# Squared latent tiles summed on VectorE before one product with ones, instead of one product with ones per tile

## The chip, the cores and the metric

The kernel runs on one core of one Trainium2 chip. The metric is the device time of one execution in microseconds (us); the time of a kernel is the median of its runs. TensorE (PE) does the matrix products, VectorE (DVE) and ScalarE (ACT) the elementwise work, GpSimd (POOL) a part of the subtractions, and SyncE (SP) issues the weight loads.

## What is computed

Two models of two layers each run one after the other on 512 tokens of width 1024, all in fp32. The change lies in the first of them, in the MLA branch of `_layer`:

```python
h = x @ w_in
(c_q, c_kv, k_rope, ...) = _split_last(h, IN_SPLITS)      # c_q is 384 wide, c_kv 256
q  = (_rms_norm(c_q,  q_norm)  @ w_qb).reshape(...)
kv = (_rms_norm(c_kv, kv_norm) @ w_kvb).reshape(...)

def _rms_norm(x, g):
    y = x * rsqrt(mean(x * x, axis=-1) + 1e-6)
    return y * g
```

Beside this branch a layer has a memory attention (softmax over 256 memory tokens), a stick-breaking and a decayed-softmax attention, gates for all of them, and a merge. There are two layers of this kind, so the two norms above are computed four times in all.

## The kernel before, in words

Activations lie feature-major: a tile is 128 features by 512 tokens (128x512). c_q is three such tiles (n = 0, 1, 2) and c_kv two (n = 3, 4). A mean over features is a sum over partitions, which is done on TensorE: the square of a tile is multiplied by a 128x128 matrix of ones, and the products of all tiles of a norm are added up in one PSUM bank. After it every partition holds the sum for its token. Every other fp32 product with weights is split into three (`L1654`, `L1655`, `L1656`: low times high, high times low, high times high) in the fp32r type; the product with ones is a plain fp32 matmul, which the trace shows as two instructions.

The whole program is one list of steps, written by a planner (`plan`, line 304), and each engine's program walks this list in order and takes from it what is its own. An engine's instructions are thus in the order of the list, and a wait holds everything behind it on that engine. The planner counts a cost in ns per step (`cost_of`, line 244: 693 for one k-step of a 512-column product, that is three matmuls; 860 for a `squares` step; 0 for everything that TensorE doesn't do). `alongside` (line 687) weaves two generators by these costs: the fill (here `mla_proj`, the projections of the MLA branch) and the main (here the memory attention). It issues a main step when the fill's cost so far, times the main's total over the fill's total, has caught up with the main's cost so far, and a due time has passed. The totals come from a first run of the planner. The memory attention thus runs beside `mla_proj`, in the stage that is called `mem` here.

Line 785, `mla_proj`, in order: tiles 0 and 1 from weight `cq0` (8 k-steps each), tile 2 and then tile 3 from `cq1`; first call of the generator `normed` for q; the square of tile 3; tile 4 from `ckr`; second call; the rotary key with the forget gates (`krope`) from `ckr`; the rest of `normed` for q; `normed` for kv is started, and is called once more after each k-step of the gate projection `g0`; then `qb`, `kvb` and the rest. Each tile is followed by a step `raw` (ScalarE copies the bank to SBUF and squares it into a tile `tmp`). `normed` (line 796) puts the steps `squares` (TensorE, line 1754, the product with ones at L1761), `rroot` (ScalarE: Ln and Exp of the sum, shown as L1806), `normed` (VectorE: three operations of a Newton correction, L2139, L2142, L2144, then one multiplication per tile at L2263), and `normhi` (ScalarE rounds each tile to fp32r, L1922, and GpSimd subtracts it, L2584). Its `yield`s say between which steps the caller goes on:

```python
            put("rroot", l=l, b=b, tm=tm, dim=dim)
            yield
            tn = TN.take()
            put("normed", l=l, b=b, tm=tm, tn=tn, dim=dim, grp=grp, gain=gain)
            give(b, tm, tn)
            ready = now() + 5000
            for _ in range(40):
                if now() < ready:
                    yield
            put("normhi", l=l, grp=grp)
```

`krope` on VectorE is two operations (L2269, L2271). Further lines that the prediction names: `turn` is a group of transposes of the memory attention (L1726), `rturn` the transposes of its reciprocals (L1735), which wait for VectorE's L2404; L1692 is a logit product, L1750 a product with the values, L2376 the maximum of a logit tile, L1817 a load of an activation table, L1826 and L2175 or L2570 the splitting of a weight chunk. L2247 is VectorE's part of a gate.

Of the kernel before, what the change touches and what calls it, by code (L numbers as in the profile page):

```python
# [303 lines left out]
def plan(known):  # L304
# [480 lines left out]
    def mla_proj(l, box):  # L785
        sq = []

        def take_tile(w, c0):
            b = yield from gemm("fm", w, c0, c0 + 128, ("x", l), range(8))
            tm = TM.take()  # L790
            put("raw", l=l, n=len(sq), b=b, tm=tm)
            give(b)
            sq.append(tm)
            yield

        def normed(grp, dim, gain):
            b = GR[0].take()
            for n in grp:
                put("squares", l=l, n=n, b=b, tm=sq[n], first=n == grp[0], last=n == grp[-1])
                give(sq[n])  # L800
            tm = TM.take()
            put("rroot", l=l, b=b, tm=tm, dim=dim)
            yield
# [9 lines that stand above are left out]
        w = wnext("cq0")  # L813
        yield from take_tile(w, 0)
        yield from take_tile(w, 128)
        wdone(w)
        w = wnext("cq1")
        yield from take_tile(w, 0)
        b = yield from gemm("fm", w, 128, 256, ("x", l), range(8))
        wdone(w)  # L820
        put("rawcopy", l=l, n=3, b=b)
        give(b)
        norm_q = normed((0, 1, 2), 384, "qn")
        next(norm_q)
        sq.append(TM.take())
        put("rawsquare", l=l, n=3, tm=sq[3])
        yield
        w = wnext("ckr")
        yield from take_tile(w, 0)
        next(norm_q, None)  # L830
        b = yield from gemm("fm", w, 128, 256, ("x", l), range(8))
        put("krope", l=l, b=b)
        give(b)
        rest_of(norm_q)
        wdone(w)
        norm_kv = normed((3, 4), 256, "kvn")
        next(norm_kv)
        yield
        g0 = gate("g0", l, "mla", l)
        for x in g0:  # L840
            if x is not None:
                box["u"] = x
            next(norm_kv, None)
            yield
        rest_of(norm_kv)
        w = wnext("qb")
        for c in range(2):
            b = yield from gemm("fm", w, 128 * c, 128 * c + 128, ("nq", l), range(3))
            put("qnope", l=l, c=c, b=b)
            give(b)  # L850
            tick()
            yield

        def turn_rope(part, src):
            b, t2 = GR[0].take(), TM.take()
            put("rope1", l=l, part=part, src=src, b=b, tm=t2)
            give(b, t2)

        b = yield from gemm("fm", w, 256, 384, ("nq", l), range(3))
        tm = TM.take()  # L860
        put("qb", l=l, b=b, tm=tm)
        give(b)
        wdone(w)
        turn_rope("k", None)
        yield
        w = wnext("kvb")
        for c in range(2):
            b = yield from gemm("fm", w, 128 * c, 128 * c + 128, ("nkv", l), range(2))
            put("knope", l=l, c=c, b=b)
            give(b)  # L870
            tick()
            yield
        turn_rope("q", tm)
        give(tm)
        for i in range(4):
            b = yield from gemm("kvv", w, 256, 512, ("nkv", l), range(2), tile=i)
            put("mlav", l=l, i=i, b=b)
            give(b)
            tick()
            yield  # L880
        wdone(w)
        e_ = TM.take()
        put("foxgate", l=l, e=e_)
        give(e_)
# [356 lines left out]
    for l in range(2):  # L1241
        box, tail = {}, iter(())
        run(project(l, "A", box, first))
        first = {}
# [112 lines left out]
def build(nc, ctx, a, out):  # L1357
# [184 lines left out]
    def tensor_program(e):  # L1542
# [50 lines left out]
        for s in STEPS:  # L1593
# [160 lines left out]
            elif k == "squares":  # L1754
                b = s["b"]
                w.wait_ge(d_tail, d_tail.at("tail"))
                if s["first"]:
                    for g, v in b.free():
                        w.wait_ge(g, v)
                w.wait_ge(a_fn, a_fn.at(("square", s["tm"])))  # L1760
                t = e.matmul(bank(b), C("ones"), tm(s["tm"]), start=s["first"], stop=s["last"])  # L1761
                t.then_inc(aux.sem, aux.mark(b, ends=(s["tm"],)))
            elif k == "rope1":
                b = s["b"]
                w.wait_ge(d_tail, d_tail.at("tail"))
                for g, v in b.free():
                    w.wait_ge(g, v)
                if s["part"] == "k":
                    w.wait_ge(v_copy, v_copy.at(("krope", s["l"])))
                    src = kp  # L1770
                else:
                    w.wait_ge(v_copy, v_copy.at(("qb", s["src"])))
                    src = tm(s["src"])
                t = e.matmul(bank(b), C("rot16"), src, start=True, stop=True)
                t.then_inc(aux.sem, aux.mark(b))
            elif k == "rope2":
                b = s["b"]
                for g, v in b.free():
                    w.wait_ge(g, v)
                w.wait_ge(a_copy, a_copy.at(("pair", s["src"])))  # L1780
                t = e.matmul(bank(b), C(ROT[s["br"]][0]), tm(s["src"]), start=True, stop=True)  # L1781
                t.then_inc(aux.sem, aux.mark(b))
            elif k in ("qsquares", "dsquares"):
                b = s["b"]
                for g, v in b.free():
                    w.wait_ge(g, v)
                sq = s["sq"] if k == "qsquares" else s["ta"]
                w.wait_ge(a_fn, a_fn.at(("square", sq)))
                t = e.matmul(bank(b), C("bones"), tm(sq), start=True, stop=True)
                t.then_inc(aux.sem, aux.mark(b))  # L1790
            elif k == "vturn":
                b = s["b"]
                for g, v in b.free():
                    w.wait_ge(g, v)
                w.wait_ge(a_copy, a_copy.at(("vcopy", s["tm"])))
                for i in range(4):
                    c = slice(128 * i, 128 * i + 128)
                    t = e.transpose(bank(b)[:, c], tm(s["tm"])[:, c], C("ident"))
                t.then_inc(feat.sem, feat.mark(b, ends=(s["tm"],)))
# [331 lines left out]
    def vector_program(e):  # L2131
# [34 lines left out]
        for s in STEPS:  # L2166
# [82 lines left out]
            elif k == "mkv" and s["n"] == 1:  # L2249
# [3 lines left out]
                    w.wait_ge(heado, heado.at(("heado", 0, "mem", 1)))  # L2253
                t = e.tensor_copy(mv[:, c, :], bank(b)[:, 0:256])
                t.then_inc(v_copy.sem, v_copy.mark(("mkv", l, 1, c), ends=(b,)))
            elif k == "normed":
                l, x = s["l"], tm(s["tm"])
                w.wait_ge(d_par1, d_par1.at("par"))
# [503 lines left out]
```

## Time and profile before

| | |
|---|---|
| runs | 1453.92, 1451.4, 1452.3 us; median 1452.3 |
| profiled execution | 1448.79 us, span 1447.0 |
| mean granted clock of TensorE | 0.988 |
| busy: PE, DVE, ACT, POOL | 95%, 59%, 50%, 26% of the span |

The span goes from the first to the last instruction; 1.8 us of the profiled execution lie outside it. PE's busy share counts a matmul from its start to its modelled end, and such matmuls overlap: two 512-column matmuls of the same kind start about 0.23 us apart and are 0.39 us long each. So the start times are what to read, not the durations. The granted clock is 1.00 at 2.4 GHz and 0.50 at 1.2 GHz.

### The profile page before, as it was taken

The page shows a single profiled execution, that of the slowest core. Times are in us where ns is not written, and L with a number is a line of the kernel's source. Part 1 is how long each engine was busy: PE and PEld are TensorE (multiplying, and loading weights), DVE is VectorE, ACT ScalarE, POOL GpSimd, SP SyncE. Part 2 cuts the span into 40 slices and gives each one's busy share as a digit, 9 for nine tenths or more (in the row PEclk, how much of TensorE's full clock was granted, in tenths as well). Part 3 has the DMA queues.
Part 4 walks back from the last instruction along what each step waited for, and adds up shares of the span by engine and source line. Part 5 has one row for each costly group of instructions (what it writes and reads, how often), then busy time and mean ns, then how long its engine had stood idle before and what let it go on. Part 6 is the DMA issues. An engine that isn't in the chain of part 4 may idle for free.

```text
span 1447.0 us, 20166 instructions
## 1 busy us (share of the span) xinstructions
PE 1378.0 (95%) x7530; PEld 1061.5 (73%) x7530; DVE 858.3 (59%) x1505; ACT 728.8 (50%) x1557; POOL 379.6 (26%) x273
## 2 busy tenths in 40 slices
PE   7999999999989999999998899999899999999897
PEld 7867688778787677887776876766667876766665
DVE  4655536557562553365587685458756665558655
ACT  4554447555244554566554464445444554536443
POOL 2232131345132321313564111421102111421111
PEclk9999999999999999999999999999999999999999
DMA  6413551126343221112255523612323342520311
GB/s 235 117 31 92 113 142 48 50 72 226 102 161 62 57 89 59 59 48 66 77 218 174 131 65 67 124 59 52 102 67 88 103 102 64 113 65 23 117 52 59
DMA packets 185895, 135.67 MB, mean 94 GB/s; under 512 B 91334, under 2 KB 166726, under 8 KB 185798
## 3 DMA queue, kind: packets, MB, share of 16 engines
q1 hardware_dynamic: 182022, 120.22, 30.8%
q10 hardware_dynamic: 3776, 14.16, 2.6%
q8 instruction: 61, 1.00, 0.3%
q14 instruction: 36, 0.29, 0.1%
HBM read 122.03 MB, written 12.32 MB: 93 GB/s over the span
## 4 chain that ended last, share of the span: by engine, by line
PE 74%; DVE 13%; ACT 9%; issue 2%; POOL 1%; DMA 0%; DVEq 0%; ACTq 0%; POOLq 0%
PE pb L1654 19%; PE pb L1656 18%; PE pb L1655 18%; PE pb L1750 5%; PE pb L1692 5%; PE pb L1726 4%; ACT prob L1806 4%; ACT tmp L1806 2%; DVE wl L2175 2%; DVE prob L2426 2%; ACT wh L1826 1%; PE pb L1781 1%; PE pb L1735 1%; PE pb L1698 1%; DVE small L2412 1%
## 5 line engine op out<-in xcount | busy, mean ns | idle before, releaser
L2570 POOL TENSOR_TENSOR wl<-wr,wh 128x512 fp32r<-128x512 f32 x178 | 251.4, 1413 | 724.8 <-ACT wh L1826 721.0
L1654 PE MATMUL pb<-xh,wl 128*128 128x512 f32 (+1 forms) x880 | 349.5, 397 | 6.4 <-DVE wl L2175 3.1
L1656 PE MATMUL pb<-xh,wh 128*128 128x512 f32 (+1 forms) x880 | 326.0, 370 | 0.0
L1655 PE MATMUL pb<-xl,wh 128*128 128x512 f32 (+1 forms) x880 | 325.8, 370 | 0.0
L2175 DVE TENSOR_TENSOR wl<-wr,wh 128x512 fp32r<-128x512 f32 x208 | 171.5, 827 | 173.3 <-ACT wh L1826 173.0
L1826 ACT CAST wh<-wr 128x512 fp32r<-128x512 f32 (+1 forms) x386 | 220.1, 606 | 34.0 <-PE pb L1656 15.1
L1654 PEld LDWEIGHTS pb<-xh,wl 128*128 128x128 f32 x880 | 168.4, 191 | 62.0 <-issue 31.8
L1656 PEld LDWEIGHTS pb<-xh,wh 128*128 128x128 f32 x880 | 168.1, 191 | 29.1
L1655 PEld LDWEIGHTS pb<-xl,wh 128*128 128x128 f32 x880 | 168.9, 192 | 23.2 <-issue 2.9
L1806 ACT ACTIVATE tmp<-pb,cst 128x512 f32<-128x512 f32 (+3 forms) x128 | 83.0, 648 | 81.5 <-PE pb L1656 35.5
L1654 PE MATMUL pb<-wh,xl 128*128 128x256 f32 (+1 forms) x320 | 108.9, 340 | 10.0 <-DVE wl L2175 7.9
L1726 PEld LDWEIGHTS pb<-cst,prob 128*128 128x128 f32 x768 | 93.3, 142 | 31.0 <-issue 11.4
L1726 PE MATMUL pb<-cst,prob 128*128 128x128 f32 x768 | 111.7, 276 | 4.1 <-DVE small L2401 2.2
L2059 ACT COPY prob<-pb 128x512 f32<-128x512 f32 (+3 forms) x128 | 61.4, 480 | 106.2 <-PE pb L1726 105.6
L1806 ACT ACTIVATE prob<-prob,small 128x512 f32<-128x512 f32 (+3 forms) x128 | 75.9, 594 | 72.0 <-DVE small L2389 71.9
L1656 PE MATMUL pb<-wh,xh 128*128 128x256 f32 (+1 forms) x320 | 105.3, 329 | 0.0
L1655 PE MATMUL pb<-wl,xh 128*128 128x256 f32 (+1 forms) x320 | 105.2, 329 | 0.0
L1806 ACT ACTIVATE prob<-pb,small 128x512 f32<-128x512 f32 (+1 forms) x96 | 58.2, 614 | 90.5 <-DVE small L2412 50.9
L2591 POOL TENSOR_TENSOR yl<-tmp,yh 128x512 fp32r<-128x512 f32 x28 | 36.1, 1291 | 244.1 <-ACT yh L2071 240.5
L2447 DVE COPY prob<-pb 128x512 f32<-128x512 f32 (+3 forms) x128 | 70.0, 551 | 43.3 <-PE pb L1726 42.8
L1654 PE MATMUL pb<-wh,yl 128*128 128x512 f32 (+1 forms) x176 | 69.5, 395 | 8.7 <-DVE wl L2175 7.0
L1654 PEld LDWEIGHTS pb<-wh,xl 128*128 128x128 f32 x320 | 61.3, 192 | 21.6 <-DVE wl L2175 8.2
(200 smaller groups left out, 2326.5 us busy)
## 6 DMA issues: line engine op xcount, KB each, us to landing
wr<-w_in SPq DMA_DIRECT2D x39, 1024.0 KB, 5.4
wr<-w_out SPq DMA_DIRECT2D x14, 1024.0 KB, 5.0
wr<-w_in SPq DMA_DIRECT2D x48, 256.0 KB, 4.6
wr<-w_branch SPq DMA_DIRECT2D x48, 128.0 KB, 2.3
x<-prob SPq DMA_DIRECT2D x12, 512.0 KB, 3.2
wr<-w_mem_kv SPq DMA_DIRECT2D x4, 1024.0 KB, 5.8
prob<-x ACTq DMA_DIRECT2D x2, 2048.0 KB, 11.0
wr<-w_out SPq DMA_DIRECT2D x16, 256.0 KB, 4.2
```

The source lines that it names most:

```text
L1654: e.matmul(ps, ll, rh, start=start, stop=False)
L1655: e.matmul(ps, lh, rl, start=False, stop=False)
L1656: t = e.matmul(ps, lh, rh, start=False, stop=stop)
L1692: t = e.matmul(bank(b)[:, 0:128 * (hi - lo)], lhs, rhs, start=True, stop=br != "mla")
L1726: t = e.transpose(bank(b)[:, c], probs(p)[:, c], C("ident"))
L1750: t = e.matmul(bank(b)[64 * half:64 * half + 64, lo:hi], v_[:, j, vc:vc + 64], turns(s["t"][half])[:, j, lo - 256 * ih:hi - 256 * ih], sta ...
L1806: return e.activation(o, i, f, bias=C("zero", 0, i.shape[0]) if bias is None else bias, scale=scale, **kw)
L1826: e.copy(wh[:, j % 2, c0:c1], wr[:, j % 2, c0:c1]).then_inc(w_hi.sem, w_hi.mark((j, c)))
L2059: t = e.copy(turns(t_)[:, lo:hi, 128 * i:128 * i + 128], bank(b)[:, 0:128 * (hi - lo)].rearrange("p (j c) -> p j c", c=128))
L2175: t = e.tensor_tensor(wl[:, j % 2, c0:c1], wr[:, j % 2, c0:c1], wh[:, j % 2, c0:c1].bitcast(F32), ALU.subtract)
L2447: t = e.tensor_copy(turns(t_)[:, lo:hi, 128 * i:128 * i + 128], bank(b)[:, 0:128 * (hi - lo)].rearrange("p (j c) -> p j c", c=128))
L2570: t = e.tensor_tensor(wl[:, j % 2, c0:c1], wr[:, j % 2, c0:c1], wh[:, j % 2, c0:c1].bitcast(F32), ALU.subtract)
```

## The change

`normed` first has VectorE add the other squared tiles of the group into the first one (steps `sqsum`: two for q, one for kv), and gives the caller its turn; when it is called again, it puts one `squares` step for the sum, and `rroot`. Everything behind it in `normed` thus comes one call later than before. The product with ones waits for VectorE's sum and no longer for ScalarE's square.

```diff
         def normed(grp, dim, gain):
+            for n in grp[1:]:
+                put("sqsum", tm=sq[grp[0]], add=sq[n])
+                give(sq[n])
+            yield
             b = GR[0].take()
-            for n in grp:
-                put("squares", l=l, n=n, b=b, tm=sq[n], first=n == grp[0], last=n == grp[-1])
-                give(sq[n])
+            put("squares", l=l, b=b, tm=sq[grp[0]])
+            give(sq[grp[0]])
             tm = TM.take()
             put("rroot", l=l, b=b, tm=tm, dim=dim)
             yield
...
             elif k == "squares":
...
-                if s["first"]:
-                    for g, v in b.free():
-                        w.wait_ge(g, v)
-                w.wait_ge(a_fn, a_fn.at(("square", s["tm"])))
-                t = e.matmul(bank(b), C("ones"), tm(s["tm"]), start=s["first"], stop=s["last"])
+                for g, v in b.free():
+                    w.wait_ge(g, v)
+                w.wait_ge(v_fn, v_fn.at(("sqsum", s["tm"])))
+                t = e.matmul(bank(b), C("ones"), tm(s["tm"]), start=True, stop=True)
...
+            elif k == "sqsum":
+                x = tm(s["tm"])
+                w.wait_ge(a_fn, a_fn.at(("square", s["tm"])))
+                w.wait_ge(a_fn, a_fn.at(("square", s["add"])))
+                w.wait_ge(v_fn, v_fn.n)
+                t = e.tensor_tensor(x, x, tm(s["add"]), ALU.add)
+                t.then_inc(v_fn.sem, v_fn.mark(("sqsum", s["tm"]), ends=(s["add"],)))
```

## Rows read from the trace of the kernel before

**Rows 1.** The page: busy time of the engines, and the chain that ended last.
```profile
PE 1378.0 (95%) x7530; PEld 1061.5 (73%) x7530; DVE 858.3 (59%) x1505; ACT 728.8 (50%) x1557; POOL 379.6 (26%) x273
...
PE 74%; DVE 13%; ACT 9%; issue 2%; POOL 1%; DMA 0%; DVEq 0%; ACTq 0%; POOLq 0%
```
**Rows 2.** The instructions of L1761, the products with ones: count, ns min/median/max.
```profile
L1761 PE MATMUL pb<-tmp,cst x20: 590/592/593, 77.2 to 488.0; 128*128 128x512 f32 x20
```
**Rows 3.** Timeline of PE, layer 0: start us, length us, instructions merged, idle before.
```profile
77.24 2.73 PE L1761 MATMUL pb<-tmp,cst 128*128 128x512 f32 x6
79.90 1.13 PE L1692 MATMUL pb<-tbias,setB 64*128 64x256 f32 x8
...
91.82 0.38 PE L1726 MATMUL pb<-cst,prob 128*128 128x128 f32 x2
...
92.73 0.38 PE L1726 MATMUL pb<-cst,prob 128*128 128x128 f32 x2
...
94.34 1.88 PE L1761 MATMUL pb<-tmp,cst 128*128 128x512 f32 x4
96.06 0.60 PE L1726 MATMUL pb<-cst,prob 128*128 128x128 f32 x4
```
**Rows 4.** Timeline of DVE, layer 0, around both norms.
```profile
87.00 1.07 DVE L2142 SCALAR_TENSOR_TENSOR scr<-scr,tmp 128x512 f32<-128x512 f32 x1
...
88.83 2.08 DVE L2263 SCALAR_TENSOR_TENSOR setB<-setB,par,tmp 128x512 f32<-128x512 f32 x3
...
94.54 0.74 DVE L2269 TENSOR_SCALAR fz<-pb,par 36x512 f32<-36x512 f32 x1 [1.88 <-PE pb L1656]
95.21 0.67 DVE L2271 COPY setB<-pb 128x512 f32<-128x512 f32 x1
...
97.74 0.69 DVE L2139 SCALAR_TENSOR_TENSOR scr<-pb,tmp 128x512 f32<-128x512 f32 x1 [0.84 <-ACT tmp L1806]
...
99.91 1.42 DVE L2263 SCALAR_TENSOR_TENSOR setB<-setB,par,tmp 128x512 f32<-128x512 f32 x2
```
**Rows 5.** Timeline of DVE: a 128x512 fp32 operation of two SBUF tiles.
```profile
54.89 0.69 DVE L2208 TENSOR_TENSOR setA<-setA 128x512 f32<-128x512 f32 x1 [1.40 <-ACT setA L1806]
```
**Rows 6.** The chain of waits in layer 0 from the kv norm to `rturn`.
```profile
96.26 0.70 ACT tmp L1806
...
104.74 1.04 ACT yh L1922 x2
105.80 1.28 ACT L1817
107.09 0.69 ACT u L1806
...
109.55 0.63 PE pb L1735 x4
```
**Rows 7.** Timeline of PE: `rturn` of both layers, layer 1's kv products, a later wait.
```profile
105.79 0.60 PE L1726 MATMUL pb<-cst,prob 128*128 128x128 f32 x4
109.55 0.63 PE L1735 MATMUL pb<-cst,tmp 128*128 128x128 f32 x4 [3.16 <-DVE tmp L2404]
...
486.72 1.88 PE L1761 MATMUL pb<-tmp,cst 128*128 128x512 f32 x4
...
501.92 0.63 PE L1735 MATMUL pb<-cst,tmp 128*128 128x128 f32 x4 [3.16 <-DVE tmp L2404]
...
811.79 0.58 PE L1654 MATMUL pb<-xh,wl 128*128 128x256 f32 x1 [2.86 <-DVE wl L2175]
```
**Rows 8.** Stretches: us, busy us (x instructions) of PE, PEld, DVE, ACT, POOL, clock, DMA, GB/s.
```profile
811.00:818.00 7.00, 6.21 (x30) 6.21 (x30) 6.34 (x17) 3.67 (x8) 0.00 (x0) 0.51 0.85 174
98.00:110.00 12.00, 8.84 (x49) 6.75 (x47) 7.25 (x16) 6.67 (x17) 4.01 (x4) 1.00 0.00 0
```
**Rows 9.** Timeline of POOL in layer 0: a weight chunk and the `normhi` of q.
```profile
85.90 1.62 POOL L2570 TENSOR_TENSOR wl<-wr,wh 128x512 fp32r<-128x512 f32 x1
...
94.19 4.00 POOL L2584 TENSOR_TENSOR yl<-setB,yh 128x512 fp32r<-128x512 f32 x3 [1.53 <-ACT yh L1922]
```

## The prediction

> **What bounds the kernel now.** I began with the page: TensorE is busy 95% of the span and carries 74% of the chain that ended last, so a TensorE product that goes is worth something unless another engine ends the stretch it stands in [rows 1]. Then the line of the products with ones: 20 instructions, two to a product, so ten products: three for q and two for kv in each of two layers [rows 2]. Then the timelines around them. In layer 0 the q products start at 77.24 and the next work at 79.90, with no idle time around them; the kv products go from 94.34 to 96.06, again without a gap on either side [rows 3]. So far TensorE is the bound. Last I read the chain behind the kv products: it leaves TensorE at 96.26 for ScalarE's Ln and Exp and comes back only at 109.55, at `rturn`, where TensorE has waited 3.16 us [rows 6, 7]. Between the end of the kv products and `rturn` the time is thus set by ScalarE and VectorE, 109.55 - 96.06 = 13.5 us of it. Layer 1 repeats this to the hundredth: kv products at 486.72, `rturn` at 501.92, after 3.16 us [rows 7].
>
> **What is removed.** Of q's three products two go: (79.90 - 77.24) x 2/3 = 1.77 us. Of kv's two one goes: (96.06 - 94.34) / 2 = 0.86 us [rows 3]. All of it lies on the path: 2.63 us per layer, 5.3 in all. If all the rest were free, the kernel would gain that.
>
> **What is added for q.** Two additions on VectorE, at 0.69 us each by the row of two SBUF tiles [rows 5]. The one product that is left stands 8 k-steps (8 x 0.68 us) further on, behind the whole of tile 4. The sum is ready long before, so this costs nothing. It would cost at most these 1.4 us if VectorE were late; but VectorE idles between its jobs here. ScalarE's square of tile 3 has to wait for the first addition, since it takes over the tile that this one frees; nobody needs that square for over 5 us.
>
> **What the later step does.** This is the heart of the matter. The second call of `normed` for q now puts `squares` and `rroot`, and the third part (`normed` on VectorE, `normhi`) comes only when `mla_proj` asks for the rest, behind `krope`. There the planner's clock stands still, and all of it is put at once. VectorE's order behind the end of the `krope` product then is: two operations of `krope`, three Newton operations, three multiplications for q, and only then the one addition for kv. Before, the six q operations ran beside the `krope` product, from before 87.0 to 90.9 [rows 4], where VectorE had time. TensorE's order behind the same product, followed through the planner's costs: one `turn` of two transposes, one k-step of `g0`, and then the kv product, which waits for the addition. (The pacing changes a little: three steps of 860 less in the fill's total raise the ratio, and a few main steps come one k-step earlier. I followed them to the end of the stage and found none that comes to a bank or a copy too early.)
>
> Price, layer 0. TensorE comes to the kv product at 94.34 plus a turn and a k-step, which by the spacing of two such turns is 92.73 - 91.82 = 0.91 us [rows 3]: at 95.25. VectorE starts `krope` at 94.54, and its copy ends at 95.88; the three Newton operations take 99.91 - 97.74 = 2.17, the three multiplications 2.08, the addition 0.69 [rows 4, 5], with steps of 0.03 between them: the sum is there at about 100.9. TensorE waits 100.95 - 95.25 = 5.7 us, with everything behind it in its order: a turn, the gate products, the next logits. ScalarE is held too, at the first `normhi` cast until the first q tile is there (98.8), and then runs at VectorE's pace to 100.8; behind it there are only the root of kv, which waits for TensorE anyway, a copy and a weight chunk that is due 15 k-steps later. Bounds of this wait: 5.5 us if each step is as short as its shortest row, and 6.5 if two operations are stretched as L2142 was, to 1.07 from 0.69, while GpSimd worked at 85.90 [rows 4, 9]. I take 5.7, since GpSimd's `normhi` work [rows 9] can start only at 99.4, and touches only the last operation or two.
>
> Here a rule of the Trainium skill speaks against the change ("GPSIMD Engine Reference", 1. Specifications): GpSimd's SBUF interfaces are shared with VectorE and contend with VectorE instructions that have two SBUF inputs. The addition and the multiplications are such instructions. By the rule the last two would take up to 1.07 us, and the wait 6.5 instead of 5.7; by the plain rows it stays at 5.7. That row of 1.07 agrees with the rule, but `krope` and L2139 ran at their usual length beside GpSimd's 94.19 to 98.19.
>
> **Clock.** Behind a wait of 2.86 us at 811 us TensorE was granted 0.51 over the next 7 us; the wait of 3.16 us before `rturn` left it at 1.00 [rows 7, 8]. A wait of 5.7 us is longer than both, so I expect the lower of the two levels, 1.2 GHz, behind it. The kv product then takes 1.72 instead of 0.86: +0.86 us. Whatever else TensorE does slowly until `rturn` is covered by the wait there. The bounds are 0 and, if the stretch is the whole 7 us long, the 7 x 0.49 = 3.4 us of work lost in it less the 2 us of cover: 1.4. The Trainium skill ("TensorE: Matmul & The Clock Gate", Part 1, What's actually happening) says that the throttled state is the default and activity lifts it; by that rule alone the 3.16 us wait might have dropped the clock as well, which the trace does not show.
>
> **What comes back.** Between the end of the kv product and `rturn` the chain is ScalarE's and VectorE's. One item of it moves: `normhi` for kv, 104.74 to 105.80 in the chain, stands before the gate's table load (L1817) and tanh [rows 6]. With the kv norm one k-step later and the gate's last k-step unchanged, its due time passes only when the gate step is already put, so it falls behind the tanh: the chain is shorter by 105.80 - 104.74 = 1.06 us. Bounds: 0 (it stays where it was) and 1.1; I take 1.1, since the order of steps decides it and not a duration. The wait at `rturn` goes from 3.16 to about 2, still enough for TensorE's slow clock.
>
> **Sum.** Per layer -2.63 + 5.7 + 0.86 - 1.1 = +2.8, for two layers +5.7 us (before rounding, 5.66). On the profiled execution, 1447.0 span and 1.8 around it, that is 1448.8 + 5.7 = 1454.5. The median of the runs lies 3.5 us above this execution, and the change sits in two fixed places, so I add it to the median: 1452.3 + 5.7 = 1458.0. With the least of all terms, 2 x (-2.63 + 5.5 + 0 - 1.1) = +3.5; with the most, 2 x (-2.63 + 6.5 + 1.4 - 0) = +10.5. Own range of this case: 1455.8 to 1462.8.
>
> **Rivals.**
> 1. *The wait at `rturn` swallows the new one.* TensorE waits 3.16 us there already. If `rturn`'s time hung on something that doesn't move with the kv product, each layer would lose only 5.7 - 2.63 - 3.16 = -0.1: no change, 1452.1. For it: the waits are alike in size. Against it: the chain runs through the kv root without a break, 96.26 to 109.55 [rows 6]. Chance 0.18.
> 2. *Faster: the kv sum is early.* If VectorE did the kv addition ahead of q's six operations (or these stayed beside the `krope` product), the addition would end at 95.88 + 0.7 = 96.6 or, in an order with `krope` behind it, before TensorE comes: a wait of at most 1.4 us. It decides from a wait under 2.63 us on. With none, the time is 1452.3 - 5.3 = 1447.0. For it: the step was given a turn of its own, which does spare q all waiting. Against: in the list the addition stands behind `krope` and behind the rest of q. Chance 0.09.
> 3. *Costlier: nothing comes back, and the clock stays low beyond `rturn`.* `normhi` stays in front of the tanh and a second slow stretch follows: the upper sum, 1462.8. For: 7 us at 0.51 in the trace [rows 8]. Against: cover of 2 us. Chance 0.10.
>
> That the change doesn't do what it says (the number of products) I don't count apart: 4 products with ones are sure from the diff.
>
> **Numbers.** My case has 0.63. No change is what lies within 0.2%, 2.9 us. Slower: 0.63 + 0.10 = 0.73; same 0.18; faster 0.09. The range must hold 8 in 10: from rival 1 up to the top of my own case, 1451.5 to 1463.
>
> **What would show it.** L1761 with 8 instructions. A wait of 5 to 6.5 us before the second of each layer's L1761 pairs, released by VectorE's new addition; right ahead of that addition L2139, L2142, L2144 and three L2263 without a gap behind L2271. The granted clock near 0.5 behind it. `normhi` (L1922) behind the gate's tanh, and `rturn` with some 2 us of wait. No wait at q's L1761. I am wrong if the addition for kv stands ahead of L2139 on VectorE, or if `rturn` minus the end of the kv product is not near 12.4 us.

## The result, and the profile after

The kernel after takes 1458.81 us (median of 7 runs, 1455.17 to 1463.64), the kernel before beside it 1452.19 (7 runs, 1448.98 to 1453.92). The ratio is 1.0055, 95% interval 1.0041 to 1.0070: some 8 us slower (5.9 to 10.2); the two medians as they stand differ by 6.6. The forecast was 1458.0. That it lies so close is in part luck: two errors cancel, as the last experiment and the sum below show. The profiled execution of after took 1459.74 us, its span 1457.9, at a mean granted clock of 0.986 (before: 0.988).

The code behind the change stands a few lines lower in after: L1761 is L1763, L1735 is L1738, L2404 is L2413, L2263 (the multiplication) is L2272; L2139, L2142, L2144 are L2141, L2144, L2146. VectorE's new addition is L2263, so L2263 names two different things in the two kernels.

The page of after, busy time and chain [against rows 1]:
```profile
PE 1376.9 (94%) x7518; PEld 1061.2 (73%) x7518; DVE 864.0 (59%) x1511; ACT 730.0 (50%) x1557; POOL 381.0 (26%) x273
...
PE 74%; DVE 14%; ACT 9%; issue 2%; POOL 1%; DMA 0%; ACTq 0%; DVEq 0%; POOLq 0%
```
TensorE has 12 instructions less and VectorE 6 more, as planned. The page shows little else; the waits have to be read from the timelines. The products with ones, L1763 [against rows 2]:
```profile
L1763 PE MATMUL pb<-tmp,cst x8: 590/826/1193, 86.5 to 498.9; 128*128 128x512 f32 x8
```
Eight instructions, four products. A median of 826 and a maximum of 1193 ns against 592 say that half of them ran on a slower clock. TensorE's timeline (start us, length us, instructions merged, idle before) of both layers [against rows 3 and 7]:
```profile
86.55 1.02 PE L1763 MATMUL pb<-tmp,cst 128*128 128x512 f32 x2
...
93.39 0.38 PE L1729 MATMUL pb<-cst,prob 128*128 128x128 f32 x2
...
100.92 2.04 PE L1763 MATMUL pb<-tmp,cst 128*128 128x512 f32 x2 [6.44 <-DVE tmp L2263]
102.75 0.63 PE L1729 MATMUL pb<-cst,prob 128*128 128x128 f32 x2
...
115.82 0.63 PE L1738 MATMUL pb<-cst,tmp 128*128 128x128 f32 x4 [1.64 <-DVE tmp L2413]
...
497.87 2.05 PE L1763 MATMUL pb<-tmp,cst 128*128 128x512 f32 x2 [6.45 <-DVE tmp L2263]
499.71 0.63 PE L1729 MATMUL pb<-cst,prob 128*128 128x128 f32 x2
...
512.78 0.63 PE L1738 MATMUL pb<-cst,tmp 128*128 128x128 f32 x4 [2.06 <-DVE tmp L2413]
```
q's product doesn't wait. kv's waits 6.44 us, then takes 1.84 us instead of 0.86; `rturn` (L1738) waits 1.64 instead of 3.16. What the kv product waits for, on VectorE [against rows 4]:
```profile
93.59 0.74 DVE L2278 TENSOR_SCALAR fz<-pb,par 36x512 f32<-36x512 f32 x1 [1.90 <-PE pb L1659]
94.26 0.67 DVE L2280 COPY setB<-pb 128x512 f32<-128x512 f32 x1
94.86 0.67 DVE L2141 SCALAR_TENSOR_TENSOR scr<-pb,tmp 128x512 f32<-128x512 f32 x1
95.57 0.69 DVE L2144 SCALAR_TENSOR_TENSOR scr<-scr,tmp 128x512 f32<-128x512 f32 x1
96.29 0.69 DVE L2146 SCALAR_TENSOR_TENSOR tmp<-scr,tmp 128x512 f32<-128x512 f32 x1
97.02 2.08 DVE L2272 SCALAR_TENSOR_TENSOR setB<-setB,par,tmp 128x512 f32<-128x512 f32 x3
99.13 1.64 DVE L2263 TENSOR_TENSOR tmp<-tmp 128x512 f32<-128x512 f32 x1
...
114.68 1.00 DVE L2413 COPY tmp<-small 128x512 f32<-128x512 f32 x1
```
The two `krope` operations, q's three Newton operations and three multiplications, then the addition: this is the order that was followed. The addition takes 1.64 us, not 0.69. GpSimd's timeline says what stands beside it, and beside L2413 as well [against rows 9]:
```profile
98.57 4.67 POOL L2593 TENSOR_TENSOR yl<-setB,yh 128x512 fp32r<-128x512 f32 x3 [6.70 <-ACT yh L1924]
...
114.13 2.68 POOL L2593 TENSOR_TENSOR yl<-setB,yh 128x512 fp32r<-128x512 f32 x2 [1.22 <-ACT yh L1924]
```
ScalarE, at the end of the chain to `rturn` [against rows 6]: the table load and the tanh, and the `normhi` casts of kv now behind them:
```profile
111.50 1.28 ACT L1819 ACT_TABLE_LOAD   x1
112.79 0.69 ACT L1808 ACTIVATE u<-pb,cst 128x512 f32<-128x512 f32 x1
113.38 1.12 ACT L1924 CAST yh<-setB 128x512 fp32r<-128x512 f32 x2
```
And the stretches of after around the wait, with the granted clock behind the five engines' busy time [against rows 8]:
```profile
100.00:104.00 4.00, 3.08 (x6) 1.82 (x7) 1.10 (x2) 0.97 (x2) 3.08 (x3) 0.50 0.00 0
...
106.00:116.00 10.00, 8.36 (x45) 6.32 (x44) 6.42 (x13) 6.18 (x16) 3.08 (x3) 1.00 0.00 0
```
The clock is at 0.50 behind the wait until about 105 us and at 1.00 again on the way to `rturn`.

### The profile page after: what moved, and what is told of

The parts are those of the page before. It is cut to its first block, busy times and chain, and to the rows that moved or that the text cites. A ratio compares the mean times of both kernels' runs of the same rounds, so it can differ in the third digit from the quotient of the medians.

```text
span 1457.9 us, 20156 instructions
## 1 busy us (share of the span) xinstructions
PE 1376.9 (94%) x7518; PEld 1061.2 (73%) x7518; DVE 864.0 (59%) x1511; ACT 730.0 (50%) x1557; POOL 381.0 (26%) x273
## 4 chain that ended last, share of the span: by engine, by line
PE 74%; DVE 14%; ACT 9%; issue 2%; POOL 1%; DMA 0%; ACTq 0%; DVEq 0%; POOLq 0%
PE pb L1657 19%; PE pb L1659 17%; PE pb L1658 17%; PE pb L1753 5%; PE pb L1695 5%; PE pb L1729 4%; ACT prob L1808 4%; ACT tmp L1808 2%; DVE prob L2435 2%; DVE wl L2177 2%; ACT wh L1828 1%; PE pb L1783 1%; PE pb L1738 1%; PE pb L1701 1%; PE pb L1619 1%
```

## The experiments

Eleven more kernels were timed beside before, and before was profiled a second time (e12). The letters of the theories are those of the expectations. Throughout, A is: *the place of the steps in the orders of the engines costs the time (of the kv addition, and of q's operations that stand ahead of it), the addition itself does not.* e1, e2, e3 and e6 ran beside one set of 17 executions of before (median 1451.27), e4, e5, e7 and e8 beside another of 27 (1449.94), e9 to e11 beside a third of 19 (1451.88), so the ratios compare better than the medians. Times are medians; "layers" are two stretches of the profile, from a `rturn` before the change's place to one behind it (75.42 to 155.39 and 322.31 to 547.68 us in before), each less the same stretch of before. The last column puts their sum against the second profile of before (e12). Each pair of layers is read from one execution, and TensorE's clock behind `rturn` can add some 1.5 us to a layer in one execution and not in another (see e12 and the last section).

| kernel | median us | ratio [95%] | layers 0, 1 | sum against e12 |
|---|---|---|---|---|
| after | 1458.81 | 1.0055 [1.0041, 1.0070] | +5.5, +4.8 | +6.4 |
| e1 later only | 1458.56 | 1.0050 [1.0032, 1.0067] | +5.6, +6.4 | +8.2 |
| e2 sum only | 1457.87 | 1.0044 [1.0028, 1.0061] | +6.0, +3.9 | +6.1 |
| e3 q's rest beside | 1454.99 | 1.0022 [1.0011, 1.0032] | +3.4, +4.0 | +3.6 |
| e4 both sums early | 1450.78 | 1.0009 [1.0000, 1.0018] | +2.1, +1.5 | -0.2 |
| e5 `normhi` 7500 | 1449.55 | 1.0000 [0.9992, 1.0009] | -0.2, +0.9 | -3.1 |
| e6 q's `normhi` later | 1461.79 | 1.0072 [1.0056, 1.0088] | +7.4, +6.7 | +10.2 |
| e7 busy wait | 1460.21 | 1.0075 [1.0061, 1.0089] | +6.0, +4.4 | +6.5 |
| e8 e4 and 7500 | 1452.23 | 1.0016 [1.0007, 1.0025] | +1.2, +1.7 | -1.0 |
| e9 added as squared | 1447.72 | 0.9972 [0.9960, 0.9983] | +0.1, -1.0 | -4.7 |
| e10 e9 and 9500 | 1444.10 | 0.9953 [0.9941, 0.9966] | -1.0, -2.0 | -6.8 |
| e11 before and 9500 | 1448.26 | 0.9980 [0.9970, 0.9990] | -1.1, +0.1 | -4.8 |
| e12 before again | 1453.82 | one execution | +2.5, +1.3 | 0 |

### e1: the later steps alone

```diff
         def normed(grp, dim, gain):
+            if len(grp) == 2:
+                yield
             b = GR[0].take()
...
             yield
+            if len(grp) == 3:
+                yield
             tn = TN.take()
```


> The products with ones stay one per tile, as before; only the steps behind them come one call later: the Newton operations and multiplications of q behind krope, and the two kv products behind the first k-step of g0. Theory A (the order of the steps is what costs, and the wait for the sum is one of its faces): TensorE has no wait before its kv products, but ScalarE is held at q's normhi until VectorE has done q's six operations, and kv's root stands behind that; kv's Newton operations begin some 4.5 us later than before, the gate's tanh comes out of kv's normhi's way (up to -1.1) and 0.7 us of products are done earlier: +2.5 to +3.5 us per layer, 1457 to 1459 us where before has 1452.2. Theory B (only the wait of TensorE for VectorE's sum costs): within 1 us of before, 1451 to 1453.

Ratio 1.0050, as slow as after, although no product is saved and no addition made. There is hardly a wait at the kv products, as they need only ScalarE's squares; it stands elsewhere. TensorE, then VectorE, then ScalarE of this kernel:
```profile
96.54 1.98 PE L1765 MATMUL pb<-tmp,cst 128*128 128x512 f32 x4 [0.52 <-DVE setB L2275]
...
114.96 0.63 PE L1739 MATMUL pb<-cst,tmp 128*128 128x128 f32 x4 [3.45 <-DVE tmp L2408]
```
```profile
98.57 2.08 DVE L2267 SCALAR_TENSOR_TENSOR setB<-setB,par,tmp 128x512 f32<-128x512 f32 x3
...
102.68 0.69 DVE L2143 SCALAR_TENSOR_TENSOR scr<-pb,tmp 128x512 f32<-128x512 f32 x1 [1.69 <-ACT tmp L1810]
103.40 1.63 DVE L2146 SCALAR_TENSOR_TENSOR scr<-scr,tmp 128x512 f32<-128x512 f32 x1
```
```profile
99.36 1.94 ACT L1926 CAST yh<-setB 128x512 fp32r<-128x512 f32 x3 [5.24 <-DVE setB L2267]
101.21 0.68 ACT L1810 ACTIVATE tmp<-pb,cst 128x512 f32<-128x512 f32 x1
```
ScalarE's Ln for kv (101.21) is queued behind q's three casts, and they wait for VectorE's multiplications. So kv's root, and with it `rturn`, is late by the same VectorE chain; TensorE pays in several small waits and a longer one at `rturn`. Shown: the later steps, without any wait for a sum, cost 7.3 us in all; a part of it is slow clock behind `rturn` (0.50 over some 3 us in layer 0 and 6 us in layer 1). They are not the whole cost of after, though: after has 5.3 us less of products and is no faster, so that the wait for the sum costs some 6 us more (an estimate: 8.0 + 5.3 - 7.3).

### e2: the sum alone, at the old places

```diff
                 give(sq[n])
-            yield
             b = GR[0].take()
```


> The sum on VectorE and one product, but no later step: the product stands directly behind the additions. Theory A: TensorE waits about 1.5 us for q's two additions (they stand behind the gated output's operation on VectorE) and 2.3 us for kv's one (behind krope's two operations), up to 0.9 more where GpSimd works on q's tiles beside the addition; against -2.63 removed: +1 to +2 us per layer, 1454 to 1456.5. Theory B as for A here. A third view (the additions are hidden beside other work whatever their place): 1447.

Ratio 1.0044, more than expected. Both products now wait for an addition that is put right ahead of them:
```profile
83.97 1.10 PE L1762 MATMUL pb<-tmp,cst 128*128 128x512 f32 x2 [2.60 <-DVE tmp L2262]
...
100.39 1.10 PE L1762 MATMUL pb<-tmp,cst 128*128 128x512 f32 x2 [2.33 <-DVE tmp L2262]
```
The two waits, 4.9 us, alone are more than the 2.63 saved, and in layer 1 both products also run slowly behind them (2.05 and 1.53 us long). So the later step did serve its purpose for q, whose product waits for nothing in after; it was too little for kv, and by e1 it delays the rest of q.

### e3 and e6: two ways of taking q's rest out of the way

e3 asks for q's rest after the first k-step of the `krope` product. e6 keeps it where after has it, but puts q's `normhi` some k-steps later, so that GpSimd isn't at work beside the addition.
```diff
e3
-        b = yield from gemm("fm", w, 128, 256, ("x", l), range(8))
+        b = yield from beside_norm(gemm("fm", w, 128, 256, ("x", l), range(8)), norm_q, (1,))
e6
-        rest_of(norm_q)
+        next(norm_q, None)
...
             next(norm_kv, None)
+            next(norm_q, None)
             yield
+        rest_of(norm_q)
```


> The changed kernel, but q's rest is asked for after the first k-step of the krope product, so that VectorE's six operations for q run beside that product again; the kv addition still stands behind krope's two operations. Theory A: the wait before the kv product falls from 6.4 us to about 1.2 (the addition ends some 2.1 us behind the product, TensorE arrives 0.9 behind it), the clock stays at its upper level: 1448 to 1450. If instead the loss came from the wait on the sum as such, or from the pacing of the attention steps, it stays near 1459.

> The changed kernel, but q's normhi (ScalarE's casts and with them GpSimd's subtractions) is put some five k-steps later, so that GpSimd is idle when VectorE does the kv addition. Theory C (GpSimd's work stretches the addition from 0.69 to 1.64 us): the addition takes 0.69 us, the wait falls from 6.4 to 5.5 us, and the kernel is 2 us faster than the changed one, 1456 to 1458. Rival: the addition is long for its own sake (two operands and an output in the same buffer), 1.64 again, and the time stays at 1459.

e3: ratio 1.0022, less than half of the loss. The kv product still waits 4.28 us and then runs slowly (2.04 us long). q's Newton operations begin only at 88.91 instead of 86.29, as its product comes 8 k-steps later than in before; one Newton operation is stretched to 1.66 us and a weight chunk to 1.76 beside GpSimd, and `krope` begins at 96.07 instead of 94.54. VectorE is the bound of this stretch. e6: the addition is back at its length, and the casts are in the way at another place. VectorE, then ScalarE of e6:
```profile
99.10 0.69 DVE L2265 TENSOR_TENSOR tmp<-tmp 128x512 f32<-128x512 f32 x1
```
```profile
109.87 1.67 ACT L1926 CAST yh<-setB 128x512 fp32r<-128x512 f32 x3
```
0.69 without GpSimd, 1.64 with it, at the same place and with the same neighbours: that GpSimd stretches the addition is shown. The wait falls by as much (5.49 us). But the three casts now stand in ScalarE's chain to `rturn`, which comes at 116.42 instead of 115.82, after a wait of 2.76 us instead of 1.64. At `rturn` the clock falls to 0.50 in both layers of e6 and in neither of after, and that is the larger part of its loss: the stretches behind `rturn` take 46.37 and 46.65 us instead of 45.07 and 45.16. Ratio 1.0072.

### e4 and e8: kv's addition ahead of q's rest

```diff
         next(norm_q, None)
+        norm_kv = normed((3, 4), 256, "kvn")
+        next(norm_kv)
         b = yield from beside_norm(gemm("fm", w, 128, 256, ("x", l), range(8)), norm_q, (1,))
...
-        norm_kv = normed((3, 4), 256, "kvn")
         next(norm_kv)
```
e8 is e4 with kv's `normhi` due 7500 instead of 5000 ns later.

> As the one that asks for q's rest beside the krope product, and kv's addition is put as soon as tile 4 is squared, ahead of krope; the kv product stands where it stood before the change. Theory A: no wait before any product with ones; per layer -2.63 for the products and -0.7 because one more k-step is done under the wait at rturn, whose chain is ScalarE's and VectorE's: -5.3 to -6.6 in all, 1445.5 to 1447. Rival: the gain is lost in the wait at rturn, 1449 to 1451.

> Both sums early, q's rest beside the krope product, and kv's normhi due at 7500: the version that the theories make the fastest. Sum of the two: -5.3 to -6.6 and -2.2, 1443.5 to 1445; if the relief of normhi doesn't come, as the version with both sums early.

No wait at either product and four products: all of the 5.3 us should have been kept. The ratio is 1.0009 for e4, 1.3 us slower than before (0 to 2.6). VectorE and TensorE of e4:
```profile
90.12 1.66 DVE L2159 SCALAR_TENSOR_TENSOR tmp<-scr,tmp 128x512 f32<-128x512 f32 x1
...
93.81 1.79 DVE L2190 TENSOR_TENSOR wl<-wr,wh 128x512 fp32r<-128x512 f32 x1
...
97.45 0.67 DVE L2154 SCALAR_TENSOR_TENSOR scr<-pb,tmp 128x512 f32<-128x512 f32 x1
```
```profile
92.54 1.02 PE L1776 MATMUL pb<-tmp,cst 128*128 128x512 f32 x2
...
109.24 1.09 PE L1751 MATMUL pb<-cst,tmp 128*128 128x128 f32 x4 [3.91 <-DVE tmp L2426]
```
Counted from the `rturn` ahead (74.59 here, 75.42 in before), kv's Newton begins 0.5 us later than in before [rows 4], though its product ends 1.8 us earlier: q's product and root come 8 k-steps late, so that q's operations still fill VectorE, and two operations stretched beside GpSimd (1.66 and 1.79 instead of 0.69 us) add 2.1 us to them. The gain turned into a longer wait at `rturn`, 3.91 us, and the length of that L1751, 1.09 instead of 0.63, tells that the clock had fallen. The expectation missed that VectorE follows close behind TensorE here, and GpSimd's part in it. e8 shortens the casts' part and wins nothing either (1.0016).

### e7: TensorE kept busy in the wait

```diff
+                if s["kv"]:
+                    for _ in range(6):
+                        e.matmul(bank(b), C("ones"), mask_cols("causal", 0, 512), start=True, stop=True)
                 w.wait_ge(v_fn, v_fn.at(("sqsum", s["tm"])))
```


> The changed kernel with six products of ones with a constant (about 5.3 us) put before each kv product, into the bank that this one then starts anew; their result isn't used. They lie inside the wait of 6.4 us. Theory: TensorE's clock then stays at 1.00, the kv product takes 0.9 instead of 1.8 us, and since the chain to rturn starts at its end, the kernel is 1.8 to 2 us faster than the changed one though TensorE does more, 1456 to 1457. Rival: the slow clock was covered, or the added products push the kv product back: 1459 or more.

TensorE in both layers, and the stretch behind the first `rturn`:
```profile
100.82 1.12 PE L1766 MATMUL pb<-tmp,cst 128*128 128x512 f32 x2 [0.42 <-DVE tmp L2266]
...
114.82 0.63 PE L1738 MATMUL pb<-cst,tmp 128*128 128x128 f32 x4 [2.93 <-DVE tmp L2416]
...
512.98 0.63 PE L1738 MATMUL pb<-cst,tmp 128*128 128x128 f32 x4 [2.91 <-DVE tmp L2416]
```
```profile
114.00:118.00 4.00, 3.18 (x12) 2.66 (x13) 2.89 (x4) 0.24 (x1) 1.73 (x2) 0.73 0.21 32
```
The clock holds at the kv product, and in layer 0 `rturn` comes 1.0 us earlier. But the wait at `rturn` is longer too, 2.93 instead of 1.64 us, and behind it the clock falls, where no wait covers it: the next `rturn` comes 46.62 us later instead of 45.07, 1.5 us lost for 1.0 won. In layer 1, after a wait of 2.91 us, it stays at 1.00, and the layer is 0.4 us shorter than in after. The ratio, 1.0075 (1.0061 to 1.0089), shows no gain over after's 1.0055 (1.0041 to 1.0070). So the 0.98 us of the kv product was not won back this way; that the slow stretch behind `rturn` is the whole reason is shown for one layer of one execution only.

### e9: each addition soon behind its square

```diff
+        def added(n0, n):
+            put("sqsum", tm=sq[n0], add=sq[n])
+            give(sq[n])
+            yield
...
         def normed(grp, dim, gain):
-            for n in grp[1:]:
-                put("sqsum", tm=sq[grp[0]], add=sq[n])
-                give(sq[n])
-            yield
             b = GR[0].take()
...
-        yield from take_tile(w, 0)
-        b = yield from gemm("fm", w, 128, 256, ("x", l), range(8))
+        yield from take_tile(w, 0, added(0, 1))
+        b = yield from beside_norm(gemm("fm", w, 128, 256, ("x", l), range(8)), added(0, 2), (4,))
...
-        b = yield from gemm("fm", w, 128, 256, ("x", l), range(8))
+        b = yield from beside_norm(gemm("fm", w, 128, 256, ("x", l), range(8)), added(3, 4), (1,))
```
`beside_norm` steps its second argument once after the k-steps named in its third, counted from 1; what the expectation calls the fifth and the second k-step are the code's fourth and first.

> The kernel after, with each addition put soon behind the square it needs and no later step: tile 1's addition is put after the fifth k-step of tile 1's successor product, tile 2's after the fifth k-step of tile 3's product, kv's after the second k-step of the krope product; both products with ones stand where the kernel before has them. Theory A (the sum itself is cheap; what costs is its place in VectorE's order): no wait of more than 0.1 us at either product with ones, the wait at rturn near 3.2 us as before, the granted clock at 1.00 there as before, and -2.63 us per layer of the removed products, 5.3 us in all: ratio about 0.9964 (-5 us against the kernel before, range -3.5 to -6). Rival D (the stretch is bound by VectorE all along, as the run with both sums early suggested): the removed products are paid back at rturn, whose wait grows by 0.9 us per layer and with it the clock falls behind it: ratio 0.999 to 1.001. Rival E (GpSimd and VectorE's two-input additions get in each other's way): each addition takes 1.64 instead of 0.69 us and pushes VectorE's q operations back, ratio 0.998.

Ratio 0.9972, 4.1 us faster than before (2.5 to 5.8), with the same additions and products as after. TensorE and VectorE:
```profile
92.72 1.02 PE L1776 MATMUL pb<-tmp,cst 128*128 128x512 f32 x2
...
108.23 1.09 PE L1751 MATMUL pb<-cst,tmp 128*128 128x128 f32 x4 [3.65 <-DVE tmp L2426]
```
```profile
89.56 1.77 DVE L2276 TENSOR_TENSOR tmp<-tmp 128x512 f32<-128x512 f32 x1
...
96.26 1.57 DVE L2157 SCALAR_TENSOR_TENSOR scr<-scr,tmp 128x512 f32<-128x512 f32 x1
```
No wait at the products, and the gain lies in the range: A holds. e9 differs from after in two things at once, the place of the additions and that no step is deferred; which of the two is worth how much it doesn't tell. Part of the gain goes where rivals D and E said. The wait at `rturn` grows to 3.65 us (3.44 in layer 1), where the expectation had 3.2, and the clock falls behind it in both layers, where it had 1.00. In layer 0 kv's addition takes 1.77 us beside GpSimd, and kv's second Newton operation, now early enough to meet GpSimd's subtraction for q, takes 1.57 us.

### e5, e10 and e11: `normhi` of kv later

The term "what comes back" by itself, with due 7500 (e5) and 9500 (e11) in the kernel before, and with 9500 in e9 (e10):
```diff
-            ready = now() + 5000
+            ready = now() + (5000 if len(grp) == 3 else 9500)
```
(and 60 instead of 40 tries for 9500).

> The kernel before with one edit: the due time of kv's normhi is 7500 instead of 5000, so that it falls behind the gate's tanh and the reciprocals. Theory: ScalarE's two casts (1.1 us) leave the chain to rturn in both layers, its wait falls from 3.16 to about 2.1 us: -2.2 us, 1450. Rival: something else on the way to rturn is then late (GpSimd's work slows VectorE's copy, as in the changed kernel, where the relief was only 0.3 us): 1451.5 to 1452.5.

> The kernel before with one change: kv's normhi due 9500 instead of 5000 ns later. Due 7500 gave nothing, because GpSimd's subtraction then fell on VectorE's L2404, which took 1.28 instead of 0.44 us. If that collision was the whole reason, the relief of 1.06 us per layer is now seen: L2404 at 0.43 us, wait at rturn 2.1 instead of 3.16, ratio 0.9985 (-2.1 us). If it was not (TensorE is at its own pace right behind rturn or the casts hold up other work of ScalarE), the ratio stays at 1.000.

> The run with each addition behind its square, and kv's normhi due 9500 instead of 5000 ns later, so that its two casts stand behind rturn's work on ScalarE and GpSimd's subtraction behind VectorE's L2404. Theory A with relief: the chain from the kv product to rturn loses the casts (1.06 us), L2404 keeps 0.43 us since GpSimd isn't at work then, the wait at rturn falls to about 2.1 us; -1.1 us per layer more than the same kernel without it: ratio about 0.995 (-7.3 us). Rival: the casts behind rturn hold up ScalarE's exponentials of the next logits, or the kvb products wait for the parts; then it is equal to or slower than the kernel without it (ratio 0.9964 or more).

VectorE and GpSimd of e5, VectorE of e11, then TensorE's `rturn` in layer 1 of e5 and of e11:
```profile
108.03 1.27 DVE L2404 COPY tmp<-small 128x512 f32<-128x512 f32 x1
```
```profile
107.75 2.68 POOL L2584 TENSOR_TENSOR yl<-setB,yh 128x512 fp32r<-128x512 f32 x2 [1.50 <-ACT yh L1922]
```
```profile
108.43 0.43 DVE L2404 COPY tmp<-small 128x512 f32<-128x512 f32 x1
```
```profile
501.29 1.08 PE L1735 MATMUL pb<-cst,tmp 128*128 128x128 f32 x4 [2.97 <-DVE tmp L2404]
```
```profile
499.92 0.63 PE L1735 MATMUL pb<-cst,tmp 128*128 128x128 f32 x4 [2.13 <-DVE tmp L2404]
```
With 7500 the casts leave ScalarE's chain, but GpSimd's subtraction lands on the copy that `rturn` waits for: 1.27 instead of 0.43 us, ratio 1.0000. With 9500 both are out of the way, `rturn` waits 2.12 us, ratio 0.9980 (0.9970 to 0.9990), which holds the 0.9985 expected. In layer 1 of both profiled executions the clock falls behind `rturn`, after 2.97 us in e5 and after 2.13 us in e11 (there 0.50 from some 1 us behind `rturn` on, for some 3 us), which is why their second layers show no gain (+0.9 and +0.1). e10 does both and is the fastest kernel here: 0.9953 against before, 6.8 us (4.9 to 8.6), and each of its executions (1443.76 to 1445.62) is faster than the fastest of before beside it (1447.93).

### e12: the kernel before once more

> The kernel before, unchanged, profiled a second time. Its 19 executions beside the last runs took 1447.9 to 1449.1 us (six, mean granted clock 0.988 to 0.991) or 1451.2 to 1453.2 us (thirteen, 0.984 to 0.989), and the profile of before that all comparisons of traces use is of the lower group (1448.79). Theory: in the upper group TensorE's clock falls to 0.50 behind a wait which the lower one gets through at 1.00; the wait of 3.16 us at rturn is a candidate. If this execution is of the upper group (1451 or more) and the theory holds, one or both rturns are followed by a stretch at 0.50, worth 0.8 to 1.2 us each, and the other places that differ from the first profile are clock dips too. If it is of the lower group, it repeats the first profile within 1 us at every landmark and the candidate stays open.

1453.82 us, so this execution is of the upper group. TensorE at `rturn` of both layers, and the stretches behind the first:
```profile
110.48 1.09 PE L1735 MATMUL pb<-cst,tmp 128*128 128x128 f32 x4 [3.17 <-DVE tmp L2404]
...
505.10 0.98 PE L1735 MATMUL pb<-cst,tmp 128*128 128x128 f32 x4 [3.16 <-DVE tmp L2404]
```
```profile
109.00:112.00 3.00, 1.52 (x6) 1.46 (x7) 2.23 (x7) 0.44 (x2) 0.79 (x1) 0.55 0.09 15
112.00:116.00 4.00, 4.00 (x12) 2.58 (x13) 0.29 (x1) 0.00 (x0) 0.00 (x0) 0.50 0.74 251
```
The same kernel, the same wait to the hundredth [against rows 7 and 8], and this time the clock falls to 0.50 behind it, in both layers. It costs 2.5 us in layer 0 (48.36 against 45.84 us from this `rturn` to the next) and 1.6 in layer 1 (47.34 against 45.76), of which the layer as a whole keeps 1.3. The two layers are 3.8 of the 5.0 us by which this execution's span is longer; another 0.9 lies ahead of the first `rturn`, at 76.34 instead of 75.42. So the profile that the prediction was made from is one of the luckier executions of before: of the 19 beside e9 to e11, six took 1447.9 to 1449.1 us, thirteen 1451.2 to 1453.2. The split is clear in that set only; the 17 and the 27 executions beside the other kernels are not split so: all but the longest of each set lie between 1447.7 and 1453.5 us, with no gap above 1.1. That the other longer executions have the same cause is likely but seen in this one only. It also ran on another chip than the kernels compared with it, so that a difference between chips isn't excluded. In the table, the layers against e12 come much nearer to the ratios of e9 to e11 (-4.7, -6.8 and -4.8 us, measured -4.1, -6.8 and -2.9) than those against the first profile (-0.9, -3.0, -1.0). For e5 they don't: -3.1 by its profile, and 0 measured. But the executions of before beside e4, e5, e7 and e8 have a median of 1449.94, only 1.1 us above the first profile, and there the first profile is the nearer measure for e5 (+0.7) and e7 (+10.4, measured 10.9), while e4 and e8 (measured +1.3 and +2.3) lie between the two.

## Why the prediction was right

The sign and the main mechanism, TensorE's wait for a kv addition that stands behind q's operations, came out as forecast. The median did too, but in part by luck: the terms of the sum did not all hold. The terms of one layer, with layer 1's measured ones (from the `rturn` at 322.31 us of before, 327.81 of after, to that at 547.68 and 557.94):

| step | predicted | measured | how |
|---|---|---|---|
| products removed | -2.63 | -2.63 | half the instructions or less; 1.77 ahead of the kv product, 0.86 at it |
| work moved ahead of the kv product | 0 | +0.97 | TensorE comes to it 163.61 us after the `rturn` instead of 164.41: -0.80 = -1.77 + 0.97 |
| wait for the addition | +5.7 | +6.45 | the timeline |
| slow clock at the product | +0.86 | +0.98 | 499.71 - 497.87 = 1.84, less 0.86 |
| chain to `rturn` | -1.1 | -0.41 | 512.78 - 499.71 = 13.07 instead of 13.48 |
| behind `rturn` | 0 | -0.60 | 45.16 instead of 45.76 us to the next one, which holds one k-step less (29 products of `xh` and `wh` instead of 30) |
| sum | +2.8 | +4.8 | |

- *VectorE's and TensorE's orders* were right to the step. e1 shows that the later steps cost 7.3 us without any addition, e9 that with the additions placed early no product waits for them.
- *The wait* was mis-sized by 0.75 us. The addition takes 1.64 us beside GpSimd; I had taken 0.69 and kept up to 6.5 as a bound. The rule of the Trainium skill that I weighed and set aside ("GPSIMD Engine Reference", 1. Specifications: shared SBUF interfaces) was right, and e6 measures it at 0.95 us for this operation. The counter-evidence I took from the rows was none: of the two `krope` operations and L2139, which kept their length beside GpSimd, none has two SBUF inputs, since all three read a product from PSUM (`pb` in their rows).
- *What comes back* was 0.41 instead of 1.1. The casts did move behind the tanh; but GpSimd's subtraction moved with them, onto L2413 (1.00 instead of 0.43 us). I took the order of the steps for the whole answer and didn't ask what the moved cast sets off on the next engine. e5 and e11 separate the two: nothing, and 2.9 us. By the prediction's own test this part was wrong: from the end of the kv product to `rturn` it is 13.07 us in both layers (115.82 - 102.75), not near 12.4.
- *A missing term*: the turn and the k-step that pass ahead of the kv product lie ahead of a stretch that a chain sets, so they push `rturn` back by 0.97, and only 0.60 returns behind it, where one k-step less is left to do.
- *The clock*: size and place were right in after, 0.98 us for a predicted 0.86. But "the wait of 3.16 us before `rturn` left it at 1.00" was read from one execution; e12 shows the opposite for the same wait. The Trainium skill ("TensorE: Matmul & The Clock Gate", Part 1, What's actually happening: throttled is the default) would have warned of this, and e12's 0.50 behind the wait of 3.17 us agrees with it.
- *Why 1458.0 was still met.* By layer 1's measured terms, after is about 2 x 4.8 = 9.5 us above the first profile of before: 1448.8 + 9.5 = 1458.3. I had 5.7 there, 3.8 too little, and then added it to a median 3.5 us above that profile. The median of before very likely holds the slow clock behind `rturn`, which after's profiled execution, 0.9 us above its median, hasn't (1.64 and 2.06 us of wait, and a clock of 1.00 behind both); that surcharge should not have been carried over. Neither is shown beyond the profiled executions. The two errors cancel.
- *The rivals.* Wait swallowed at `rturn`: no, `rturn` moved by 6.3 us in layer 0. kv sum early: not in after, but it is what e4 and e9 built. e4 got 1450.78 from it, since VectorE was then the bound; e9 got 1447.72, near the 1447.0 that I gave it. Costlier: not as written, since `normhi` did move behind the tanh; but less than half of its relief came back, and the second slow stretch, absent from after's profile, stands behind `rturn` in e1, e2, e6 and e7.

## What to carry to other kernels

Ask of each step that a change defers what stands in line with it on every engine, and who stands behind that: here the deferred calls cost 7.3 us by themselves (e1), against 5.3 us of removed products, and putting each addition soon behind its square, with no call deferred, turned a loss of 0.55% into a gain of 0.28%. Work moved out from under a wait that another engine's chain sets is not free, and a wait may cost the clock behind it; shorten that chain too, and follow the moved instruction to the engine that it feeds. Where a kernel's executions differ by as much as the effect, learn which of them the profile shows before adding a difference to the median.

## What the runs showed of the hardware

- VectorE operations of two SBUF tiles, and copies from SBUF to SBUF, grew by 0.6 to 1.1 us where they met a GpSimd subtraction (1.28 us each when alone): 0.69 to 1.57, 1.64, 1.77 and 1.79 us (e9, after, e9, e4), 0.43 to 1.00 and 1.27 (after, e5). Operations that read PSUM kept theirs: 0.74, 0.67 and 0.69 us beside GpSimd's 94.19 to 98.19 in before. Not each one that met GpSimd was hit: the three multiplications of q in after ran 0.5 us into GpSimd's work (98.57) and kept their 2.08 us.
- The same wait of 3.16 us left TensorE at 2.4 GHz in one execution and at 1.2 GHz in another. Within one execution too: 2.97 us at `rturn` kept the clock in layer 0 of e5 and lost it in layer 1, and so did 2.12 and 2.13 us in e11; in e7 2.93 us lost it and 2.91 us kept it. The waits of 1.10 to 2.06 us at `rturn` (after, e2 in layer 1, e3) kept it, those of 3.44 to 3.97 us (e1, e4, e6, e8, e9) lost it. In between, the length of the wait alone doesn't decide it. One slow stretch behind `rturn` cost 1.4 to 2.5 us (e5, e12).
- Keeping TensorE busy with six products of constants held the clock at 1.00 through the wait (e7, 94 to 102 us), at no gain in the time of the kernel.
